# First modulation and first four projection units of a two-block kernel, split into halves by features

## The reference, cut to what matters

```python
mod = c @ w_ada + b_ada                      # [1, 1024] @ [1024, 3072]
shift, scale, gate = split(mod, 3)
h = rmsnorm(x, norm_g) * (1 + scale) + shift # x is [256, 1024]
proj = h @ w_in                              # w_in is [1024, 6152]
q_a, k_a, v_a, z_a, q_b, k_b, v_b, z_b, f_logit, g_logit = split(proj, ...)
...
mod_2 = silu(c_2) @ w_ada_2 + b_ada_2        # the second block's modulation, [1024, 6144]
```

## Time and profile before

| | us |
|---|---|
| median of 3 runs | 1429.63 (1426.18 to 1431.47) |
| the profiled execution's own time | 1427.49 |
| its span, first to last instruction | 1425.7 |
| PE busy | 1018.5 (71%) |
| DVE busy | 455.4 (32%) |
| ACT busy | 166.2 (12%) |
| POOL busy | 59.1 (4%) |
| moved by DMA | 503.76 MB, mean 353 GB/s |

### The profile page before, as it was taken

How to read it: one execution, slowest core, us unless ns; L and a number is a source line. 1 busy time by engine, 2 the same in 40 slices (tenths; PEclk the granted TensorE clock), 3 DMA queues, 4 the chain that set the end, 5 groups by cost and what they waited for, 6 DMA issues and landing times.

```text
span 1425.7 us, 14737 instructions
## 1 busy us (share of the span) xinstructions
PE 1018.5 (71%) x5931; PEld 527.4 (37%) x5931; DVE 455.4 (32%) x932; ACT 166.2 (12%) x409; POOL 59.1 (4%) x94
## 2 busy tenths in 40 slices
PE   4999999999998986656456465564656636566366
PEld 1867688655456442222122121221212212122121
DVE  1356477344467452122121120211202112121121
ACT  0133123002234110000000000000000000000000
POOL 4000211011020000000000000000000000000000
PEclk8999999999999988888688787887878878788788
DMA  9946666555637799999999999999999999999996
GB/s 350 376 176 236 237 236 225 198 130 168 226 114 284 293 350 423 429 427 427 428 430 427 428 429 429 428 428 429 429 427 428 428 429 427 429 428 429 427 427 262
DMA packets 81518, 503.76 MB, mean 353 GB/s; under 512 B 5638, under 2 KB 11038, under 8 KB 57412
## 3 DMA queue, kind: packets, MB, share of 16 engines
q1 hardware_dynamic: 78752, 496.22, 85.2%
q0 software_dynamic: 2656, 6.93, 2.1%
q10 hardware_dynamic: 68, 0.02, 0.0%
HBM read 501.54 MB, written 1.61 MB: 353 GB/s over the span
## 4 chain that ended last, share of the span: by engine, by line
PE 49%; DMA 42%; DVE 3%; SPq 3%; issue 1%; ACT 1%; DVEq 0%
DMA flex<-in_w_dram 30%; PE ps L564 11%; DMA arena<-in_w_dram 10%; PE ps L575 9%; PE ps L1069 9%; PE ps L1097 7%; DMA ring<-in_w_ada_dram 2%; PE ps L1042 2%; SPq L399 2%; PE ps L1114 1%; SPq L406 1%; DMA ring<-in_w_in_dram 1%; PE ps L952 1%; PE ps L696 1%; PE ps L597 1%
## 5 line engine op out<-in xcount | busy, mean ns | idle before, releaser
L1069 PE MATMUL ps<-ring,arena 128*32 128x512 f32 x1024 | 258.1, 662 | 98.0 <-DMA arena<-in_w_dram 97.0
L1069 PE MATMUL ps<-arena 128*32 128x512 f32 x768 | 257.7, 663 | 90.4 <-DMA flex<-in_w_dram 88.2
L1097 PE MATMUL ps<-arena 128*32 128x512 f32 x370 | 142.3, 727 | 65.9 <-DMA flex<-in_w_dram 65.2
L1097 PE MATMUL ps<-ring,arena 128*32 128x512 f32 x496 | 140.7, 729 | 63.2 <-DMA arena<-in_w_dram 63.2
L564 PE MATMUL ps<-flex,ring 128*128 128x256 f32 x640 | 145.9, 385 | 2.2 <-ACT flex L1176 1.5
L575 PE MATMUL ps<-ring,flex 128*128 128x512 f32 (+1 forms) x336 | 141.2, 576 | 0.7 <-DMA ring<-in_w_in_dram 0.7
L1069 PEld LDWEIGHTS ps<-ring,arena 128*32 128x32 f32 x1024 | 66.0, 120 | 178.2 <-issue 176.8
L564 PEld LDWEIGHTS ps<-flex,ring 128*128 128x128 f32 x640 | 121.1, 192 | 20.4 <-issue 3.0
L1069 PE MATMUL ps<-flex,arena 128*32 128x512 f32 x256 | 127.6, 656 | 0.0
L1069 PEld LDWEIGHTS ps<-arena 128*32 128x32 f32 x768 | 60.1, 121 | 168.6 <-issue 162.6
L2082 DVE TENSOR_TENSOR arena<-ps,grow 128x1024 f32<-128x1024 f32 x15 | 18.4, 1224 | 260.8 <-PE ps L1097 260.8
(11 more groups left out here) (403 smaller groups left out, 1053.8 us busy)
## 6 DMA issues: line engine op xcount, KB each, us to landing
ring<-in_w_dram SPq DMA_DIRECT2D x90, 2048.0 KB, 19.7
arena<-in_w_dram SPq DMA_DIRECT2D x68, 2048.0 KB, 24.1
flex<-in_w_dram SPq DMA_DIRECT2D x22, 2048.0 KB, 28.8
ring<-in_w_in_dram SPq DMA_DIRECT2D x17, 2048.0 KB, 10.5
ring<-in_w_ada_dram SPq DMA_DIRECT2D x14, 2048.0 KB, 8.9
ring<-in_w_dram SPq DMA_DIRECT2D x20, 512.0 KB, 12.9
ring<-in_w_ada_dram SPq DMA_DIRECT2D x8, 1024.0 KB, 17.8
ring<-in_w_out_dram SPq DMA_DIRECT2D x4, 2048.0 KB, 8.2
```

The costliest lines, as they stand in the source:

```text
L1069: mm = pe.matmul(ps[32 * e:32 * e + 32, g, :], xe3[:, c, 32 * e:32 * e + 32], mslot(slots[e])[:, c * W5:(c + 1) * W5], start=c == 0, stop= ...
L1097: mm = pe.matmul(ps[32 * e:32 * e + 32, 2 + n, :], actT3[:, j, 32 * e:32 * e + 32], w, start=j == 0, stop=j == 3, skip_group_check=True)
```

## The change

The columns of w_ada are loaded in two halves by features: half h holds 512 columns of the shift and the same 512 of the scale, for all 1024 inputs, in eight loads of 512 KB, into `arena` (`ada_home`) instead of the ring. After each half SP issues the matching half, by input features, of the chunks proj(0) and proj(1): the top halves (chunks c 0 to 3) after half 0, the bottom halves after half 1. After them come mod2(0), proj(2) with its wait, mod2(1), and the old loop. The ring's numbering now starts with proj(0).

On PE the modulation products have 256 columns, in four column tiles, so that tiles 0 and 1 hold this half's shift and 2 and 3 its scale. After half 0 the columns of its shift and scale are made, and the units 0 to 3 run over the chunks c 0 to 3 into the banks 0, 1, 2 and 5. The products of half 1 stand between these. Then come its columns, the transposing of rowsB, the units 0 to 3 over the chunks c 4 to 7, and the forget logits, now behind unit 3. ACT forms the features of token block 0 and DVE those of token block 1, four chunks a half. Pool waits for half 0 before its small loads, and for half 1 before the larger ones. The steps of the forget gate on ACT and DVE move from unit 0 to unit 3.

```diff
@@ -40,6 +40,7 @@
+FIRST_BANKS = (0, 1, 2, 5)
@@ -221,7 +222,8 @@
-        ada_in = [sem(f"ada_in{s}") for s in range(RING)]
+        ada_in = [[sem(f"ada_in{h}{k}") for k in range(4)] for h in range(2)]
+        top_in = [sem(f"top_in{q}") for q in range(2)]
@@ -265,7 +267,8 @@
-        chunks = [(ada[k * 2 * P:(k + 1) * 2 * P, 0:4 * W5].rearrange("(c p) n -> p c n", p=P), (2, 4 * W5)) for k in range(4)]
+        ada_home = [ar(8192 * (1 - h), 8192).rearrange("p (c s n) -> p c s n", c=DC, s=2) for h in range(2)]
+        chunks = []
@@ -382,11 +385,17 @@
-            for k in range(4):
-                sp.dma_start(cview(k)[:, 0:1, :], chunks[k][0][:, 0:1, :]).then_inc(ada_in[k], 16)
-                sp.dma_start(cview(k)[:, 1:2, :], chunks[k][0][:, 1:2, :]).then_inc(ring_in[k], 16)
-            for n in range(RING, NCH):
-                sp.wait_ge(*read_by[n - RING])
+            for h in range(2):
+                for c in range(DC):
+                    src = ada[c * P:(c + 1) * P, 0:2 * D].rearrange("p (s x) -> p s x", s=2)[:, :, h * W5:(h + 1) * W5]
+                    sp.dma_start(ada_home[h][:, c, :, :], src).then_inc(ada_in[h][c // 2], 16)
+                for q in range(2):
+                    n, c0 = proj(q), 4 * h
+                    sp.dma_start(cview(n)[:, c0:c0 + 4, :], chunks[n][0][:, c0:c0 + 4, :]).then_inc(
+                        ring_in[n % RING] if h else top_in[q], 16)
+            for n in [mod2(0), proj(2), mod2(1)] + list(range(RING + 1, NCH)):
+                if n >= RING:
+                    sp.wait_ge(*read_by[n - RING])
@@ -526,31 +535,76 @@
-            for c in range(DC):
-                pe.wait_ge((ada_in, ring_in)[c % 2][c // 2], 16)
-                for j in range(4):
-                    mm = pe.matmul(ps[32 * j:32 * j + 32, 4, :], c32[:, c * 32:(c + 1) * 32],
-                                   cview(c // 2)[:, c % 2, j * W5:(j + 1) * W5], start=c == 0, stop=c == DC - 1,
-                                   skip_group_check=True)
-                if c % 2:
+            def first_modulation(h, k):
+                pe.wait_ge(ada_in[h][k], 32)
+                for c in (2 * k, 2 * k + 1):
+                    for j in range(4):
+                        mm = pe.matmul(ps[32 * j:32 * j + 32, 4, 0:256], c32[:, c * 32:(c + 1) * 32],
+                                       ada_home[h][:, c, j // 2, (j % 2) * 256:(j % 2 + 1) * 256],
+                                       start=c == 0, stop=c == DC - 1, skip_group_check=True)
+                if k == 3:
...
-                if c in (3, 4):
-                    to_features(xn3, c - 3, c - 2)
-                if c == 5:
-                    pe.wait_ge(ld_rowsB, 16 * 11)
-                    pe.transpose(ps[:, 7, 0:116], rowsB[0:116, :], cst[0:116, C_ID:C_ID + 116]).then_inc(cols_tr, 1)
-            pe.wait_ge(mod_ok, 1)
-            for m in range(4):
-                mm = pe.matmul(ps[:, 0, m:16:4], modt[:, m * P:(m + 1) * P], cst[:, C_ID:C_ID + P:32], start=True, stop=True)
-            mm.then_inc(ab_done, 1)
-            FIRST_ORDER = [0, 4, 1, 5, 2, 6, 3, 7]
+            def first_columns(h):
+                pe.wait_ge(mod_ok, h + 1)
+                for m in range(2):
+                    mm = pe.matmul(ps[:, 4, m:8:2], modt[:, m * P:(m + 1) * P], cst[:, C_ID:C_ID + P:32],
+                                   start=True, stop=True, skip_group_check=True)
+                mm.then_inc(ab_done, 1)
...
-                if c % 4 == 3:
-                    return (hta_done, htv_done)[c // 4], 2
-                return (h0_a, h0_v)[c // 4], c % 4 + 1
+                for norm_, last_ in ((h0_a, hta_done), (h0_v, htv_done)):
+                    if c % 4 == 3:
+                        pe.wait_ge(last_, c // 4 + 1)
+                    else:
+                        pe.wait_ge(norm_, c - c // 4 + 1)
+            def first_unit(u, h, between=None):
+                n = proj(u // 2)
+                if u % 2 == 0:
+                    if h == 0:
+                        pe.wait_ge(top_in[u // 2], 16)
+                    else:
+                        chunk_in(n)
+                for m2 in range(2):
+                    if m2 and between is not None:
+                        between()
+                    o = (2 * (u % 2) + m2) * P
+                    for c in range(4 * h, 4 * h + 4):
+                        if u == 0 and m2 == 0:
+                            first_ready(c)
+                        mm = pe.matmul(ps[:, FIRST_BANKS[u], m2 * 256:(m2 + 1) * 256], cview(n)[:, c, o:o + P],
+                                       hT3[:, c, :], start=c == 0 and m2 == 0, stop=c == DC - 1, skip_group_check=True)
+                if h:
+                    mm.then_inc(unit_done[u % 2], 1)
+            for k in range(4):
+                first_modulation(0, k)
+                if k in (1, 2):
+                    to_features(xn3, k - 1, k)
+            first_columns(0)
+            first_unit(0, 0)
+            first_unit(1, 0)
+            def last_rows():
+                first_modulation(1, 2)
+                first_modulation(1, 3)
+            first_modulation(1, 0)
+            first_unit(2, 0)
+            first_modulation(1, 1)
+            first_unit(3, 0, between=last_rows)
+            first_columns(1)
+            pe.wait_ge(ld_rowsB, 16 * 11)
+            pe.transpose(ps[:, 7, 0:116], rowsB[0:116, :], cst[0:116, C_ID:C_ID + 116]).then_inc(cols_tr, 1)
+            for u in range(4):
+                first_unit(u, 1)
+            units[0] = 4
@@ -558,9 +612,7 @@
-                    for c in (FIRST_ORDER if kc_ == DC else range(kc_)):
-                        if units[0] == 1 and m2 == 0:
-                            pe.wait_ge(*first_ready(c))
+                    for c in range(kc_):
@@ -709,8 +761,8 @@
-            for u in range(26):
-                if u < 24:
+            for u in range(3, 26):
+                if 3 < u < 24:
@@ -724,7 +776,8 @@
-                if u == 0:
+                if u == 3:
+                    pe.wait_ge(colB_ok, 1)
@@ -1169,17 +1222,17 @@
-            act.wait_ge(ab_ok, 1)
-            act.wait_ge(xt_done, 2)
-            for c in range(4):
-                for i in range(TI):
-                    ins = act.activation(hT3[:, c, i * P:(i + 1) * P], ps[:, (2, 5)[i], c * P:(c + 1) * P], ACT.Identity,
-                                         scale=ab[:, c:c + 1], bias=ab[:, 8 + c:9 + c])
-                    if c == 3:
-                        ins.then_inc(hta_done, 1)
-                if c < 3:
-                    ins.then_inc(h0_a, 1)
+            def first_features(h):
+                act.wait_ge(ab_ok, h + 1)
+                act.wait_ge(xt_done, 2)
+                for c in range(4 * h, 4 * h + 4):
+                    act.activation(hT3[:, c, 0:P], ps[:, 2 + h, (c % 4) * P:(c % 4 + 1) * P], ACT.Identity,
+                                   scale=ab[:, c:c + 1], bias=ab[:, 8 + c:9 + c]) \
+                        .then_inc(hta_done if c % 4 == 3 else h0_a, 1)
+            first_features(0)
+            first_features(1)
@@ -1189,7 +1242,7 @@
-                src = ps[:, u % 2, :]
+                src = ps[:, FIRST_BANKS[u] if u < 4 else u % 2, :]
@@ -1510,24 +1563,27 @@
+            def first_features(h):
+                dve.wait_ge(mod_raw, h + 1)
+                dve.tensor_copy(modt[:, 0:256], ps[:, 4, 0:256]).then_inc(mod_ok, 1)
+                dve.wait_ge(ab_done, h + 1)
+                o = 4 * h
+                dve.tensor_tensor(ab[:, 8 + o:12 + o], ps[:, 4, 0:4], colA[:, 8 + o:12 + o], ALU.add)
+                link(dve.tensor_tensor(ab[:, o:4 + o], ps[:, 4, 4:8], colA[:, 16 + o:20 + o], ALU.add))
+                dve.scalar_tensor_tensor(ab[:, o:4 + o], ab[:, o:4 + o], 1.0, colA[:, 32 + o:36 + o], ALU.add,
+                                         ALU.mult).then_inc(ab_ok, 1)
+                dve.wait_ge(ab_ok, h + 1)
+                dve.wait_ge(xt_done, 2)
+                for c in range(o, o + 4):
+                    dve.tensor_scalar(hT3[:, c, P:T], ps[:, 5 + h, (c % 4) * P:(c % 4 + 1) * P], ab[:, c:c + 1],
+                                      ab[:, 8 + c:9 + c], ALU.mult, ALU.add) \
+                        .then_inc(htv_done if c % 4 == 3 else h0_v, 1)
+            first_features(0)
+            first_features(1)
...
-            dve.wait_ge(mod_raw, 4)
-            dve.tensor_copy(modt[:], ps[:, 4, :]).then_inc(mod_ok, 1)
-            dve.wait_ge(ab_done, 1)
-            dve.tensor_tensor(ab[:, 8:16], ps[:, 0, 0:8], colA[:, 8:16], ALU.add)
-            link(dve.tensor_tensor(ab[:, 0:8], ps[:, 0, 8:16], colA[:, 16:24], ALU.add))
-            dve.scalar_tensor_tensor(ab[:, 0:8], ab[:, 0:8], 1.0, colA[:, 32:40], ALU.add, ALU.mult).then_inc(ab_ok, 1)
-            dve.wait_ge(ab_ok, 1)
-            dve.wait_ge(xt_done, 2)
-            for c in range(4, DC):
-                for i in range(TI):
```

(11 more changed lines are left out.)

## The result

The changed kernel took 1421.6 us (median of 4 runs, 1418.44 to 1422.64) against 1430.0 before; the ratio is 0.9943, interval 0.992 to 0.9966. That is 8.2 us faster, with 4.9 to 11.4 covered; 9.2 was forecast. Two more comparisons, each on one chip with the kernel before, gave 0.9928 (0.9914 to 0.9942) and 0.9965 (0.9948 to 0.9983). Two of the three intervals don't overlap, so from chip to chip the ratio moves by more than one interval says. The mean of the three ratios is 0.9945, 7.8 us. The profiled execution took 1422.6, its span is 1420.8.

What follows compares the result with a forecast made beforehand. Nothing of the projection runs in the first 36.6 us, which 9.57 MB plus small loads set. Unit 6 moves from 86.13 to 76.9, counted in full: 1429.6 - 9.2 = 1420.4 us, range 1418 to 1423, full range 1416.5 to 1426.

Steps and rivals of the forecast that it cites:

- the signs that the prediction named for being wrong: Unit 6 starting later than 80 us, or its shift not being the shift at the kernel's end.
- 1.00 from 25 on: Sign at the kernel's start: the granted PE clock would read 1.00, that is 2.4 GHz, from 25 us on.
- Half 0 and unit 0: Start: first half landed at 16.4, its last product done at 18.3, transposes of x under the landings, unit 0 at 21.2.
- The first halves: First halves of units 0 to 3: 3.47 each at full clock, but 9.08 for units 0 and 1 together.
- Half 1: Second half of w_ada landed at 37.2, small loads mixing at no extra cost; PE wants its last quarter at about 38.8.
- the 2.4 that the prediction gives for 10 to 16: Time lost to Pool's small loads in the kernel before: 2.4 us, regained on the DMA limit if they cost only their bytes.
- The logits: Forget logits, moved from behind unit 0 to behind unit 3: the same 3.47, so unit 4 can start at 60.8.
- rival 2: Early PE stalls: half 1 comes 2.6 late and a clock fall costs 2.1; 4.5 gained, 1425.1 us; chance 0.17.
- The third chunk: Load of proj(2) before unit 4: lands at 59.9 by byte count; three more loads put the DMA limit for unit 6 at 76.1.
- The sum: Unit 6 at 76.9 by PE's path against 86.13 before, the later of two limits: 9.2 us gained, counted in full.
- SP's order: SP's load queue: proj(3) stands behind mod2(2), whose wait ends at 60.5 while mod2(1) keeps the queue busy to 65.3; slack 4.8.
- The rule on tile shapes: Early PE blocks: a change of tile shape drains PE, about 0.15 each, so a new block of products takes 1.15.

Runs made afterwards that it cites:

- e1: Changed kernel with units 0 to 3 run whole after half 1 instead of in halves: 1433.6 us, ratio 1.0031 to the kernel before.
- c_changed_again: The changed kernel measured once more without an edit: 1419.5 us, ratio 0.9928 to the kernel before.
- e2: Changed kernel without Pool's wait for half 0, so its small loads go at once: 1423.5 us, ratio 0.9951 to the kernel before.
- e3: Changed kernel with Pool's four row loads (2.1 MB) issued only after its first attention mask: 1418.4 us, ratio 0.9918 to the kernel before.
- e6: Changed kernel with the modulation weights in 32 loads of 256 KB instead of 16 of 512 KB: 1421.8 us, ratio 0.9965 to the kernel before.
- e4: Changed kernel with the forget logits split into the middle of the second halves of units 2 and 3: 1420.3 us, ratio 0.9947 to the kernel before.
- e7: Kernel before with only Pool's four row loads (2.1 MB) moved behind its first attention mask: 1428.8 us, ratio 1.0001 to the kernel before.
- e5: Changed kernel with Pool's row loads late and the logits spread, run twice: 1419.1 and 1418.3 us, ratios 0.9944 and 0.9927 to the kernel before.

## Why the prediction was right, and where it was off

**The mechanism was right, the size in part by luck.** The first four units run under the landing of half 1 (undone in e1, the time is 1433.6 against 1419.5 on the same chip), the shift passes through to 250 us unchanged and on to the last weight load, and the medians give 7.8 to 8.4 where 9.2 was forecast. But of the signs that the prediction named for being wrong both came: unit 6 started at 80.41, later than 80, and its shift of 5.7 isn't the one at the end (7.1 at the last weight load of the same traces, 8 in the medians). The clock wasn't 1.00 from 25 on either. The terms below say where the 3.5 at unit 6 went.

**Half 0 and unit 0.** Unit 0 started at 22.25, forecast 21.2. The step that failed is that the transposes lie under the landings: both sets ran after xn (12.8), the first took 1.97, and the blocks of products queued behind them. The last block ended at 20.0 instead of 18.3. Half of the columns took 0.61 instead of 0.94, the duration at the high level. In c_changed_again, with the short durations from 15.6 on, unit 0 started at 20.91.

**The first halves** took 7.15 for units 0 and 1, not 9.08. I had put the low clock here; it was at 1.00 in the changed kernel's three traces, and low in e2, e3 and e6, where they took 8.72 to 8.83. It gave back what the start had lost, and hardly matters: in e3 the second halves still began at 42.73. In the changed kernel they began at 42.57 (forecast 43.5) and ended at 56.5 (57.4).

**Half 1** was in at 38.2, forecast 37.2. The small loads mixed with it as assumed: the stretch at 249 GB/s lasts 4 us, the one at 374 ten; below 387 that is 0.68 MB or 1.8 us, where in the earlier trace rows the six us at 279 alone cost 0.8 MB against 410. That is 1.9 us; the 2.4 that the prediction gives for 10 to 16 doesn't follow from its rows. The last two small loads were issued at 38.4 to 39.8 after a pause of 5.7 and the large ones from 39.8 (41.1). Nothing waited for them.

**The logits** were the mis-sized term: 3.47 forecast, 4.52 measured, and unit 4 behind them 8.89 instead of 6.87. That is 3.1 for a fall of the clock that I had as part of rival 2 and in a different place. e3 and e4 rule the wait out as the cause and leave the stretch of 32 instructions of 8 columns. It isn't new with the change (e7). Among the nine traces with the logits in one piece it came in six (the three of the changed kernel, e3, e6, e7) and not in three (before, e1, e2); among the three traces with the logits spread it never came there. So the stretch in one piece doesn't always bring the fall, and three traces make it likely, not certain, that spreading it avoids the fall; what decides it in a single execution, the runs don't show.

**The third chunk** was wanted at 60.8 by forecast (61.0 measured) and should have been in at 59.9. It came at 62.2. The byte count of the step was right. The queues of the changed kernel, from 0 to 59.9 and from 0 to 62.2 us:

```profile
DMA packets 10538, 21.52 MB, mean 359 GB/s; under 512 B 1083, under 2 KB 1347, under 8 KB 10536
```

```profile
DMA packets 10988, 22.42 MB, mean 360 GB/s; under 512 B 1095, under 2 KB 1359, under 8 KB 10986
```

At 59.9 the 21.5 MB had moved that I counted up to proj(2), but 0.9 MB more went through before PE was released. Pool's queue had moved its 3.64 by then, so they went through SP's queue, where mod2(1) was issued right behind proj(2): the last piece of a load passes later than its place in the queue says. Why, the runs don't show. The step lacked this lag of 2.2 us. Of it 1.3 were waited for.

**The sum.** Unit 6 was 3.5 later than forecast: 1.4 from the landing of proj(2) and 2.0 from unit 4 in the low clock; the logits' own 1.05 lay inside the wait. The trace's gain at unit 6 was 5.7 instead of 9.2, and by that the forecast was a good part too high. That the medians give 8 is luck as far as the sum goes. It is consistent with a kernel before that loses to the clock in the logits, too, in some of its executions (e7), where the one whose trace I read did not, and with falls elsewhere, as the one at 262 that cost it 1.6. Within each kernel the longer executions tend to have the lower mean granted clock (of the changed kernel's four, 1422.6 at 0.874 and 1418.4 at 0.878). That this explains the whole of the difference was not tested.

**SP's order** held: proj(3) was issued at 63.3 and unit 6 didn't wait for it. **The rule on tile shapes**, weighed at 0.15 a change: a block of products for half 1 took 1.00 to 1.07 to the next operation, where I had 1.15.

## What to carry to other kernels

When a long serial load heads a kernel, look for a cut of the data that lets the first half of the consumers' sums begin under the second half of the load: here unit 4 started 12.3 earlier than with the same loads and whole units, though the cut itself added bytes ahead and broke rows into smaller pieces. Then ask what sets the end of the stage next: the byte count to that load's landing and PE's own path met within 2 us, so 2 MB of row loads, of which grow is first used at 158.6, began to hold PE up only after the change. Whether moving them pays by itself was not resolved (1.4 of 1420). A stretch of products of a few columns can cost nearly as much again in the clock (3.1 beside its own 3.47); breaking it up between wide ones is worth a try. Last, a forecast that holds in the median can still have its terms wrong: compare the times of its steps, and look for falls of the clock far from the change before trusting the difference of two traces.

## What the runs showed of the hardware that I had not expected

- The clock fell to 1.2 GHz at the end of a stretch in which PE was busy without a pause, but with products of 8 columns (e3: 3.30 busy of 3.30, then 0.52 for 6.8 us), and stayed at 2.4 GHz through a standstill of 1.84 us behind unit 3 (e4). The Trainium skill explains the gate in "TensorE: Matmul & The Clock Gate", section The HAM clock gate, by how busy the PE has been recently. In e3 the profile's busy time didn't tell of the fall, and e4 and e5 show only that it stayed away in three traces with the same products in two pieces.
- The granted clock of a stretch can read 1.00 at the start of a trace while products take their 1.2 GHz time: 10 to 16 in the changed kernel, with blocks of 1.93 against 1.07 later.
- From unit 6 to 250 us, with the granted clock at 1.00, the chain carried a shift of 5.72 through unchanged. What made traces differ in the first 290 us beside the start were single falls of the clock, 1.6 to 1.7 each (from 262 in the kernel before, from about 196 in e4).
- Alone in the queue, 2 KB pieces moved at 386 to 387 GB/s whether a load had 512 or 256 KB, against 410 to 421 with the 8 KB rows. "DMA: Bandwidth & Descriptors" of the Trainium skill, section Measured, wants 1 MiB a load for 75% of the peak, by figures for loads issued from GpSimd. With SP's queue full, no trace here shows a cost of smaller loads.
- A 2 MB load was complete some 2.2 us after as many bytes had moved as were queued up to its end (proj(2): 21.5 MB by 59.9, released at 62.2).
